# Where the norm factor enters at the recurrence layer and the last layer, and six queue orders

## The chip, the cores and the metric

The kernel runs on one core of a Trainium2 chip. The time is the device time of one execution in microseconds; less is better. Engines are named as in the profile: PE is TensorE, DVE VectorE, ACT ScalarE, POOL GpSimd, SP the sync engine, which issues most of the DMAs.

## The reference, cut to what matters

The input x is 256 tokens by 2048. A first block of two transformer layers (attention of three kinds, then an MLP) ends in an RMSNorm. A second block follows: layer 0, the recurrence layer (a gated linear recurrence beside a matrix memory), and layer 1, the last layer (a state-space layer, SSD), each behind an RMSNorm of its own, and one more RMSNorm at the end. All is in fp32.

```python
def rmsnorm_2(x, w):                        # rmsnorm is the same
    y = xf * lax.rsqrt(jnp.mean(xf * xf, axis=-1, keepdims=True) + EPS)
    return (y * w).astype(x.dtype)

def first_block(...):
    for l in range(2):
        h = rmsnorm(x, norm_mix[l]);  proj = h @ w_in[l];  ...attention...;  x = x + mix @ w_o[l]
        h = rmsnorm(x, norm_mlp[l]);  u = relu(h @ w_up[l]);  x = x + (u * u) @ w_down[l]
    return rmsnorm(x, norm_final)

def second_block(x, ...):
    # layer 0, the recurrence layer
    u = rmsnorm_2(x, e_norm) @ e_w_in;  x_l, x_m, z = split(u)
    y_l = rglru(causal_conv(x_l));  y_m = mlstm(silu(causal_conv(x_m)), x_m)
    x = x + (concat(y_l, y_m) * silu(z)) @ e_w_out
    # layer 1, the last layer
    u = rmsnorm_2(x, o_norm) @ o_w_in;  z, xbc, dt = split(u)
    y = ssd_scan(silu(causal_conv(xbc)), softplus(dt + dt_bias), ...) + d_skip * xs
    x = x + (rmsnorm_of_groups(y * silu(z)) * gnorm) @ o_w_out
    return rmsnorm_2(x, final_norm)
```

The factor of a norm is one number for each token, and the gain one for each feature. So `rmsnorm(x, g) @ W` is (x · g) @ W, with each token's row of the result times its factor.

## The kernel before, in words

**Products.** A product of two fp32 operands is made of three of rounded parts: hi·hi, hi·lo, lo·hi. Weights come from HBM in units of 1 MB (128 x 2048 numbers), each into one of four slots of `raw`. For each unit ACT writes the rounded part `whi` (`high_unit` L867, `high_parts` L983), DVE the rest `wlo` (`low_unit` L1449, `low_parts` L1442), and PE multiplies. The activations stand in `act0` and `act1`, transposed (features on the partitions, 256 tokens along the row), as a high and a low part. A group is two units and gives 256 columns of output for all tokens. It is 32 pairs of matmuls in `products()`: L2391 with `whi` against high and low activations (512 columns), L2393 with `wlo` against the high ones (256). The main part of a group lies in columns 0 to 255 of a PSUM bank pair and the minor part behind it; the eviction adds them. In the stages that add to x (`resid`) the activations are the stationary side and the weights stream (`block_products`, L2349 to L2351).

**Stages.** `stages()` (L103) lists them: for each of two layers attention and then w_up and w_down by turns, four times; `norm2`; the four parts of e_w_in, `xl`, `xm`, `zm`, `zl`, of 8 groups each; `e_mix` (heads of the matrix memory, then the product with e_w_out, 22 groups); `norm`; of o_w_in the parts `tail` (1 group), `x` (2), `z` (2), `bc` (8); then the stages `ssd` with g = 0 to 6, of 4 groups each, which project group g+1 while they compute group g of the state-space layer. After g = 3 a residual stage with the first half of o_w_out stands between them (`ssd_end`), and `ssd_out` ends the kernel with the other half.

Each engine has its own queue, written out by hand from the same list. What is written first in an engine's block is issued first, and a wait for a semaphore holds everything behind it in that queue.

**How x is turned.** At the norms inside the first block, PE transposes raw x (`turn_raw`, L2288) while the residual stage before it is still running: after each block p > 0 two turns, and the last two (6 and 7) inside group (0, 0) of the next stage. ACT writes the gained high part (`turned_high`, L973), DVE the low part (`turned_low`, L1614), and the factor enters later. At `norm2` and `norm`, it is different. There the whole factor comes first: squares of all x on ACT, their sums, roots and reciprocals on DVE and ACT (L1621 to L1643, L1173, L1174, L1178), then a diagonal matrix `xdiag` of the factors (L1646, L1647). `turn(i)` multiplies x by that diagonal, which turns and scales in one (L2278, eight matmul records a turn; i = 0 to 3 stand before the products, i = 4 to 7 inside group (0, 0)). ACT L1187 and DVE L1655 write the two parts into `act0`. `norm2` has two norms in a row (norm_final, then e_norm_2): the first gain is multiplied into x by DVE (L2030) in the last residual stage.

**Evictions.** DVE copies the minor part out of PSUM and adds it to the major part: L1958 and L1959 for `store`, L1973 and L1974 for `silu` and `gate_y`, `evacuate()` L1458 and L1459 in the `ssd` stages.

**The ssd stages on GpSimd.** In stage g GpSimd convolves the newly projected tiles (`conv_pair`, L690, L695, L698: two pairs of the stage, and in g = 1 and 2 another pair 7+g for a later one), multiplies them by their gates (`gate_pair`, L717), multiplies z by its gate (L852), and adds up the squares of the gated y for the norm over a group: `y_adds` (L707, L709) writes `osum`, which PE multiplies by ones in `y_sums` (L2331; for g = 3 and 6 PE sums straight from the squares, L2327). The squares themselves are made on ACT (`y_squares`, L908) from `gated_y` of DVE (L1509, L1515), and ACT's sigmoid of z (L880) stands before them in ACT's queue.

**The start.** ACT's queue first waits for `x_dma1`, the landing of the second part of x, issues the DMA of all gain and convolution columns (304 KB, L1120), and then evicts the first turned tiles (L973) and makes the high part of the first unit (L1123, L1125). DVE follows with L1614 and L1847, and PE begins its products at L2425.

Of the kernel before, what the change touches and what calls it, by code (L numbers as in the profile page):

```python
# [15 lines left out]
F32 = mybir.dt.float32  # L16
F32R = mybir.dt.float32r
ACT = mybir.ActivationFunctionType
ALU = mybir.AluOpType
# [84 lines left out]
def stages():  # L104

    out = [dict(kind="load")]
    for l in range(DEPTH):
# [12 lines left out]
    out.append(dict(kind="gemm", w=e_in, k0=0, c0=0, ng=8, act=0, evac="store", dst="wide_a", pre="xl"))  # L120
    out.append(dict(kind="gemm", w=e_in, k0=0, c0=D, ng=8, act=0, evac="store", dst="wide_b", pre="xm"))
    out.append(dict(kind="gemm", w=e_in, k0=0, c0=3 * D, ng=8, act=0, evac="silu", dst="wide_e", pre="zm"))
    out.append(dict(kind="gemm", w=e_in, k0=0, c0=2 * D, ng=8, act=0, evac="gate_y", pre="zl"))
    out.append(dict(kind="e_mix", w=e_out, ng=22))

    o_in, o_out = ("o_w_in_2", 0), ("o_w_out_2", 0)
    out.append(dict(kind="norm", gain=("o_norm_2", 0)))
    out.append(dict(kind="gemm", w=o_in, k0=0, c0=2 * N_DI + D + N_SSD_H - GC, ng=1, act=0, evac="store", dst="tail"))
    out.append(dict(kind="gemm", w=o_in, k0=0, c0=N_DI, ng=2, act=0, evac="store", dst="wide_b", pre="x"))
    out.append(dict(kind="gemm", w=o_in, k0=0, c0=0, ng=2, act=0, evac="silu", dst="wide_z", pre="z"))  # L130
    out.append(dict(kind="gemm", w=o_in, k0=0, c0=2 * N_DI, ng=8, act=0, evac="store", dst="wide_a", pre="bc"))
# [8 lines left out]
def number(out):  # L140
# [6 lines left out]
    for before, s in zip(out, out[1:]):  # L147
        if before.get("evac") == "resid":
            s["after_resid"] = True
        if s["kind"] != "gemm":  # L150
            continue
        if before["kind"] in ("norm", "norm2"):
            s["turns"] = True
        if before["kind"] in ("norm", "norm2") or before.get("evac") == "relu2":
# [6 lines left out]
def vector_rows():  # L161

    out = []
    for l in range(DEPTH):
# [5 lines left out]
            (("o_gnorm_2", 0), 32)]  # L170
# [95 lines left out]
def build(nc, A, out, pick=None):  # L266
# [3 lines left out]
    with ExitStack() as ctx:  # L270
# [39 lines left out]
        for key, shape in vector_rows():  # L310
            vectors[key] = (n_rows, shape)
            n_rows += shape
        columns = sb("columns", [P, n_rows])
# [33 lines left out]
        gain_row = o_raw[:, 0:8, :].rearrange("p a t -> p (a t)")  # L347
        junk = wide_1[:, 1, :, :].rearrange("p a t -> p (a t)").rearrange("p (c f) -> p c f", c=2)
        r_row = std[:, 1, :]
# [2593 lines left out]
```

## Time and profile before

| | |
|---|---|
| median of 3 runs | 3521.62 us (3520.26 to 3522.58) |
| the profiled execution | 3520.35 us |
| its span in the profile | 3518.6 us |
| PE busy | 3471.3 us, 99% |
| DVE busy | 2235.9 us, 64% |
| ACT busy | 1600.3 us, 45% |
| POOL busy | 663.0 us, 19% |
| moved from HBM | 622.13 MB, 177 GB/s over the span |

The profile is of one execution, taken by the hardware profiler. The span goes from the first to the last instruction that it recorded. PE is the engine that multiplies, and it is hardly ever idle. So the short places where it stands tell more than the shares; the view of waits lists them by the instruction that ended them.

### The profile page before, as it was taken

The numbers are of one execution on the slowest core, as the hardware profiler recorded it, in microseconds if no ns is written. First come the engines' busy times: TensorE is split into PE (matmuls) and PEld (weight loads), VectorE is DVE, ScalarE is ACT, GpSimd is POOL, SyncE is SP. The second block draws the span as 40 slices with busy tenths as digits, with TensorE's granted clock in tenths as the row PEclk, the third lists the DMA queues.
The fourth block names the chain that finished last, engine by engine and source line by source line (L and its number), as shares of the span: only waits on it lengthen the run. The fifth ranks groups of instructions, "written<-read, shape, count | busy, mean of one in ns | idle before, by whom it ended". The sixth has DMA issues, their size and how long they took to land. (4 is left out here: it accounts for less than half of the span.)

```text
span 3518.6 us, 44743 instructions
## 1 busy us (share of the span) xinstructions
PE 3471.3 (99%) x18296; PEld 2896.3 (82%) x18296; DVE 2235.9 (64%) x2155; ACT 1600.3 (45%) x1766; POOL 663.0 (19%) x551
## 2 busy tenths in 40 slices
PE   9999999999999999999999999999999999999999
PEld 7777888888887778888888878888888788777887
DVE  5666646464656677646464658866667476875786
ACT  5555333333344565333333445633454444553564
POOL 1221000000000221000000001560000069770560
PEclk9999999999999999999999999999999999999999
DMA  6344555555545354555555544455444455454554
GB/s 221 143 167 166 185 187 190 191 185 186 190 179 192 132 180 156 191 185 186 190 191 183 200 180 162 175 191 190 158 145 155 161 186 193 168 178 174 182 201 150
DMA packets 94783, 626.83 MB, mean 178 GB/s; under 512 B 10928, under 2 KB 13232, under 8 KB 21392
## 3 DMA queue, kind: packets, MB, share of 16 engines
q1 hardware_dynamic: 84096, 601.99, 46.9%
q0 software_dynamic: 3168, 11.41, 1.0%
q10 hardware_dynamic: 7344, 10.94, 0.9%
q8 instruction: 129, 2.11, 0.2%
q14 instruction: 46, 0.38, 0.0%
HBM read 622.13 MB, written 2.16 MB: 177 GB/s over the span
## 5 line engine op out<-in xcount | busy, mean ns | idle before, releaser
L2391 PE MATMUL ps<-act,whi 128*128 128x512 f32 x4384 | 1551.0, 396 | 1.8 <-DVE wlo L1442 1.8
L1442 DVE TENSOR_TENSOR wlo<-raw,whi 128x2048 fp32r<-128x2048 f32 x404 | 941.2, 2350 | 471.6 <-ACT whi L983 449.8
L2393 PE MATMUL ps<-act,wlo 128*128 128x256 f32 x4384 | 1233.7, 281 | 0.0
L2391 PEld LDWEIGHTS ps<-act,whi 128*128 128x128 f32 x4384 | 825.5, 188 | 198.8 <-issue 4.8
L983 ACT ACTIVATE whi<-raw 128x2048 fp32r<-128x2048 f32 x358 | 683.7, 1913 | 621.1 <-DMA raw<-in_w_down 309.2
L2393 PEld LDWEIGHTS ps<-act,wlo 128*128 128x128 f32 x4384 | 823.8, 188 | 0.8
L867 ACT ACTIVATE whi<-raw 128x2048 fp32r<-128x2048 f32 x211 | 402.1, 1913 | 267.9 <-DMA raw<-in_o_w_in 87.7
L1449 DVE TENSOR_TENSOR wlo<-raw,whi 128x2048 fp32r<-128x2048 f32 x165 | 389.4, 2365 | 149.3 <-ACT whi L867 149.2
L2349 PE MATMUL ps<-whi,act 128*128 128x512 f32 x1152 | 456.1, 396 | 0.0
L2350 PE MATMUL ps<-wlo,act 128*128 128x512 f32 x1152 | 455.4, 395 | 0.0
L2351 PE MATMUL ps<-whi,act 128*128 128x512 f32 x1152 | 455.4, 395 | 0.0
L2349 PEld LDWEIGHTS ps<-whi,act 128*128 128x128 f32 x1152 | 216.6, 188 | 52.6 <-issue 0.2
L2351 PEld LDWEIGHTS ps<-whi,act 128*128 128x128 f32 x1152 | 216.4, 188 | 52.5
L2350 PEld LDWEIGHTS ps<-wlo,act 128*128 128x128 f32 x1152 | 216.4, 188 | 52.2
L1239 ACT ACTIVATE act<-big 128x512 f32 (+1 forms) x64 | 40.4, 632 | 424.0 <-DVE big L1965 424.0
L728 POOL DMA_DIRECT2D wide_b<-in_bias_b x4 | 2.3, 566 | 804.6 <-DVE wide L1701 804.6
L2449 PE MATMUL ps<-act,whi 128*128 128x512 f32 x384 | 138.9, 402 | 0.0
L796 POOL DMA_DIRECT2D o_raw<-in_norm_final x1 | 0.6, 581 | 663.2 <-PE ps L2393 663.2
L1962 DVE COPY big<-ps 128x512 f32<-128x512 f32 x64 | 44.3, 692 | 122.4 <-PE ps L2393 122.4
L690 POOL TENSOR_SCALAR wide<-wide_b,columns 128x256 f32<-128x256 f32 x48 | 44.7, 938 | 352.3 <-DVE wide_b L1959 222.2
L2425 PE MATMUL ps<-whi,act 128*128 128x512 f32 x256 | 104.2, 407 | 5.3 <-DVE wlo L1847 4.4
L2451 PE MATMUL ps<-act,wlo 128*128 128x256 f32 x384 | 108.0, 281 | 0.0
(419 smaller groups left out, 4545.4 us busy)
## 6 DMA issues: line engine op xcount, KB each, us to landing
raw<-in_w_up SPq DMA_DIRECT2D x128, 1024.0 KB, 4.8
raw<-in_w_down SPq DMA_DIRECT2D x128, 1024.0 KB, 4.8
raw<-in_o_w_in SPq DMA_DIRECT2D x80, 1024.0 KB, 4.8
raw<-in_e_w_in SPq DMA_DIRECT2D x64, 1024.0 KB, 4.8
raw<-in_w_in SPq DMA_DIRECT2D x60, 1024.0 KB, 4.8
raw<-in_w_o SPq DMA_DIRECT2D x32, 1024.0 KB, 4.8
raw<-in_e_w_out SPq DMA_DIRECT2D x32, 1024.0 KB, 4.8
raw<-in_o_w_out SPq DMA_DIRECT2D x32, 1024.0 KB, 4.8
```

The source lines that it names most:

```text
L867: act.activation(whi[:, slot, :], raw[:, slot, :], ACT.Copy).then_inc(sem("hi_ready"), 1)
L983: act.activation(whi[:, slot, :], raw[:, slot, :], ACT.Copy).then_inc(sem("hi_ready"), 1)
L1442: dve.tensor_tensor(wlo[:, slot, :], raw[:, slot, :], whi[:, slot, :].bitcast(F32), ALU.subtract).then_inc(sem("lo_ready"), 1)
L1449: dve.tensor_tensor(wlo[:, slot, :], raw[:, slot, :], whi[:, slot, :].bitcast(F32), ALU.subtract).then_inc(sem("lo_ready"), 1)
L2349: pe.matmul(ps[:, b + th, :], a_hi, hi, start=(kt == 0), stop=False)
L2350: pe.matmul(ps[:, b + th, :], a_hi, lo, start=False, stop=False)
L2351: ins = pe.matmul(ps[:, b + th, :], a_lo, hi, start=False, stop=(kt == KT - 1))
L2391: pe.matmul(ps[:, b + f, :], whi[:, slot, w], a[:, kt, :, :].rearrange("p a t -> p (a t)"), start=(kt == 0), stop=False)
L2393: ins = pe.matmul(ps[:, b + f, S:2 * S], wlo[:, slot, w], a[:, kt, 0, :], start=False, stop=(kt == KT - 1))
L2425: pe.matmul(ps[:, b + th, :], a_hi, hi, start=(kt == 0), stop=False)
L2449: pe.matmul(ps[:, b + f, :], whi[:, slot, w], act0[:, kt, :, :].rearrange("p a t -> p (a t)"), start=(kt == 0), stop=False)
L2451: ins = pe.matmul(ps[:, b + f, S:2 * S], wlo[:, slot, w], act0[:, kt, 0, :], start=False, stop=(kt == KT - 1))
```

## The change

It has two parts.

**The factor enters late, also at the recurrence layer and the last layer.** The stages `norm2` and `norm` go. x is turned raw in the stage before (the last w_down for `xl`, `e_mix` for `tail`) with the gain as a column. For the recurrence layer the gains norm_final and e_norm_2 are multiplied together once, at the start. As in the first block, turns 6 and 7 stand in group (0, 0). Behind the products of group (0, 0) of `xl`, and of `tail`, PE waits for `diag` and makes a row of factors that is the same on every partition, ones x `xdiag`, in two matmuls. ACT copies it to `n_row` (which takes the place of `osum`). Each eviction of `xl`, `xm`, `zm`, `zl`, `x`, `z`, `bc` and of the `ssd` stages then multiplies by that row: DVE has a third operation; for `xl` and `xm` ACT copies the minor part (`minor_part`), so that DVE keeps two. The factor of `tail` is applied in `decay_inputs`. The factors themselves are computed beside group 0 (`paired_factors`, `single_factor`, `factor_diagonal`), between the units of ACT and DVE. GpSimd's sum of squares goes to `cos`, its gain row for norm_final to `wide_b`. The DMA of the columns stands behind turned_high(3) and waits for `x_dma3`; 8 KB with norm_final follow it.

**Six orders of the queues.** (1) The sigmoids of conv pairs 8 and 9 go on ACT from the end of their stage into the next. (2) `gate_pair(8)` and `(9)` go on GpSimd behind the products of z and `y_adds`. (3) `gated_y` stands ahead of `evacuate(g-1, 3)` on DVE. (4) `y_sums` stands later in PE's queue: in the middle of the second unit of `block_products` instead of behind the first, and in `ssd_out` inside the second instead of behind the first. (5) In `e_mix` each half of `head_products` waits for its own split, and the splits 0 and 1 are interleaved with the units. (6) `lru_scans` is made in two halves.

```diff
@@ stages
-            out[-1].update(squares=True, gain_row="norm_final", gained=True)
+            out[-1].update(squares=True, gain_row="norm_final", gained=True, turn_next=("e_norm_2", 0))
-    out.append(dict(kind="norm2", gain=("e_norm_2", 0)))
+    (xl: turned=("e_norm_2", 0), scaled_by="row"; xm, zm, zl, x, z, bc: scaled_by="row"; tail: turned=("o_norm_2", 0))
+    out.append(dict(kind="e_mix", w=e_out, ng=22, turn_next=("o_norm_2", 0)))
-    out.append(dict(kind="norm", gain=("o_norm_2", 0)))
@@ PE
                         products(s, p, c, acts[s["act"]], fresh)
+                        if s.get("turned") and s["evac"] == "store" and isinstance(p, int) and p == 0 and c == 0:
+                            pe.wait_ge(sem("diag"), 1 if s.get("pre") == "xl" else 2)
+                            pe.wait_ge(sem("x_low"), T["x_low"] + 2)
+                            for th in range(2):
+                                ins = pe.matmul(ps[:, 6, th * P:th * P + P], ones[:, :], xdiag[:, th, :], ...)
+                            ins.then_inc(sem("norm_row"), 1)
-                        if s.get("turns") and isinstance(p, int) and p == 0 and c == 0 and kt < 8 and kt % 2:
-                            turn(4 + kt // 2)
-                if k in ("norm", "norm2"):
-                    pe.wait_ge(sem("diag"), T["diag"] + 1)
-                    for i in range(4):
-                        turn(i)
+                        if s.get("ssd_end") and p == 0 and n == 1 and i == 1:        # block_products
+                            y_sums(s["ssd_end"])
-                    if s.get("ssd_end") and p == 0 and n == 0:
-                        y_sums(s["ssd_end"])
+                            if i == 1 and a == 1:                                      # ssd_out
+                                y_sums(g - 1)
-                        if i == 0:
-                            y_sums(g - 1)
-                        pe.wait_ge(sem("split"), h + 2 if part in "qk" else 5 + h)
+                        pe.wait_ge(sem("split"), h + 1 if part in "qk" else 5 + h)
+                            if a and part in "qk":
+                                pe.wait_ge(sem("split"), h + 2)
+                        if k in (24, 25, 29):                                          # e_mix
+                            i = {24: 0, 25: 2, 29: 4}[k]
+                            pe.wait_ge(sem("evacuated"), e_G0 + 16 + i)
+                            turn_raw(i, T["x_low"])
+                            turn_raw(i + 1, T["x_low"])
@@ ACT
+                    def minor_part(g):
+                        b = 2 * ((s["G0"] + g) % 2)
+                        act.wait_ge(sem("multiplied"), 2 * (s["G0"] + g) + 2)
+                        wait(act, sem("evacuated"), s["G0"] + g)
+                        act.activation(big[:, 0, :]..., ps[:, b:b + 2, S:2 * S], ACT.Copy).then_inc(sem("minor_in"), 1)
+                    def row_in():
+                        act.wait_ge(sem("norm_row"), 1 if s.get("pre") == "xl" else 2)
+                        act.activation(n_row, ps[:, 6, 0:S], ACT.Copy).then_inc(sem("norm_row_in"), 1)
+                        if s.get("pre") == "xl" and g == 0:
+                            high_unit(2 * s["G0"] + 2)
+                            gained_squares(3)
+                            high_unit(2 * s["G0"] + 3)
+                            act.wait_ge(sem("x_sum"), T["x_sum"] + 1)
+                            act.activation(rs[:, 2, :], yr[:, :], ACT.Sqrt).then_inc(sem("x_std"), 1)
+                            act.activation(rs[:, 0, :], rs[:, 1, :], ACT.Sqrt).then_inc(sem("x_r1"), 1)
+                        elif s.get("dst") == "tail":
+                            act.wait_ge(sem("x_sum"), T["x_sum"] + 1)
+                            act.activation(rs[:, 1, :], rs[:, 0, :], ACT.Sqrt, bias=eps[:, :], scale=1.0 / D)
+                            high_unit(2 * s["G0"] + 2)
+                            high_unit(2 * s["G0"] + 3)
-                        act.wait_ge(sem("x_dma1"), 32)                                 # before turned_high(0)
-                        act.dma_start(columns[:, KT:n_rows], ...)
+                        act.wait_ge(sem("x_dma3"), 32)                                 # after turned_high(3)
+                        act.dma_start(columns[:, KT:n_rows], ...).then_inc(sem("columns_in"), 16)
+                        act.dma_start(lru_c[:, 0, :], A["vectors"][:, n_rows:n_rows + KT]).then_inc(sem("final_in"), 16)
+                    if g in (2, 3):                                                    # ssd, behind high_unit(u + 5)
+                        conv_sigmoid(6 + g)
-                    if g in (1, 2):
-                        conv_sigmoid(7 + g)
@@ DVE
+                        elif s.get("pre") == "xl" and 2 * p + c == 0:
+                            gain_block(3, T["x_low"] - 6)
+                            low_unit(2 * s["G0"] + 2)
+                            paired_factors()
+                            factor_diagonal()
+                            low_unit(2 * s["G0"] + 3)
+                        elif s.get("dst") == "tail":
+                            single_factor()
+                            factor_diagonal()
+                            low_parts(s["G0"] + 1, p)
+                        if s.get("pre") in ("xl", "xm"):
+                            dve.wait_ge(sem("minor_in"), ...)
+                        elif s["evac"] != "relu2":
+                            own.then(dve.tensor_copy(t1, minor))
+                        if s.get("scaled_by"):
+                            own.then(dve.tensor_tensor(t2, major, t1, ALU.add))
+                            dve.wait_ge(sem("norm_row_in"), 1 if s["pre"] in E_AT else 2)
+                            if s.get("scaled_by"):
+                                ins = dve.tensor_tensor(to, t2, row2, ALU.mult)
@@ DVE, evacuate of the ssd stages
-                dve.tensor_tensor(to, ps[:, b:b + 2, 0:S], to, ALU.add).then_inc(sem("evacuated"), 1)
+                own.then(dve.tensor_tensor(to, ps[:, b:b + 2, 0:S], to, ALU.add))
+                dve.tensor_tensor(to, to, n_row.unsqueeze(1).broadcast_to([P, 2, S]), ALU.mult
+                                  ).then_inc(sem("evacuated"), 1)
@@ DVE, ssd, ssd_end and ssd_out
+                        gated_y(g - 1)
                         evacuate(g - 1, 3)
-                        gated_y(g - 1)
@@ POOL
-                pool.tensor_tensor(osum[:, :], squares[:, 0:S], squares[:, S:2 * S], ALU.add).then_inc(sem("s_add"), 1)
+                pool.wait_ge(sem("d_out"), 16)
+                pool.tensor_tensor(cos[:, :], squares[:, 0:S], squares[:, S:2 * S], ALU.add).then_inc(sem("s_add"), 1)
-                    if g in (1, 2):
-                        gate_pair(7 + g)
                     for m in (2 * g, 2 * g + 1):
                         ... y_adds, z ...
+                    if g in (1, 2):
+                        gate_pair(7 + g)
```

## Rows read from the trace of the kernel before

**Rows 1.** the page's busy time, share and instructions of each engine
```profile
PE 3471.3 (99%) x18296; PEld 2896.3 (82%) x18296; DVE 2235.9 (64%) x2155; ACT 1600.3 (45%) x1766; POOL 663.0 (19%) x551
```

**Rows 2.** TensorE's waits: line, releaser: us in total, times, longest us
```profile
PE ps L2331 <- POOL osum L709: 12.4, 2, 6.5
PE ps L2278 <- DVE xdiag L1647: 9.8, 2, 6.0
PE ps L2327 <- ACT staged L908: 3.7, 2, 1.9
PE ps L2391 <- DVE wlo L1442: 1.8, 3, 1.1
PE ps L2730 <- DVE act L1607: 1.8, 1, 1.8
```

**Rows 3.** timeline of the start: start us, us, engine, line, idle before
```profile
7.63 0.84 PE L2288 MATMUL ps<-ident,x 128*128 128x128 f32 x3
11.86 0.84 ACT L973 ACTIVATE act<-ps,columns 128x256 fp32r<-128x256 f32 x2 [9.18 <-DMA x<-in_x]
14.96 0.79 PE L2425 MATMUL ps<-whi,act 128*128 128x512 f32 x1 [4.41 <-DVE wlo L1847]
```

**Rows 4.** timeline, end of w_down to recurrence layer: TensorE, once VectorE
```profile
2101.18 0.40 PE L2351 MATMUL ps<-whi,act 128*128 128x512 f32 x1
...
2105.38 0.16 DVE L1628 TENSOR_REDUCE rs<-ss 128x2 f32<-128x8 f32 x1 [0.87 <-ACT big L1255]
...
2107.62 6.16 PE L2278 MATMUL ps<-xdiag,x 128*128 128x128 f32 x32 [6.05 <-DVE xdiag L1647]
2115.02 1.06 PE L2278 MATMUL ps<-xdiag,x 128*128 128x128 f32 x8
...
2129.05 0.47 PE L2391 MATMUL ps<-act,whi 128*128 128x512 f32 x1 [0.50 <-DVE wlo L1442]
```

**Rows 5.** timeline of TensorE, end of the mixing stage to the last layer
```profile
2791.95 5.36 PE L2278 MATMUL ps<-xdiag,x 128*128 128x128 f32 x32 [3.73 <-DVE xdiag L1647]
...
2811.93 0.40 PE L2391 MATMUL ps<-act,whi 128*128 128x512 f32 x1
```

**Rows 6.** timeline, attention to w_up handover: TensorE, VectorE
```profile
1381.72 1.04 PE L2288 MATMUL ps<-ident,x 128*128 128x128 f32 x8
1386.84 0.60 PE L2288 MATMUL ps<-ident,x 128*128 128x128 f32 x4
...
1392.00 4.49 DVE L1442 TENSOR_TENSOR wlo<-raw,whi 128x2048 fp32r<-128x2048 f32 x2 [0.92 <-ACT whi L983]
```

**Rows 7.** timeline of GpSimd in the recurrence stages
```profile
3008.37 2.67 POOL L709 TENSOR_TENSOR osum<-staged 128x256 f32<-128x256 f32 x1
...
3032.66 6.19 POOL L695 TENSOR_SCALAR wide<-wide_b,columns 128x256 f32<-128x256 f32 x2
...
3051.48 0.93 POOL L695 TENSOR_SCALAR wide<-wide_a,columns 128x256 f32<-128x256 f32 x2
...
3067.03 0.72 POOL L709 TENSOR_TENSOR osum<-staged 128x256 f32<-128x256 f32 x1
```

**Rows 8.** timeline of TensorE at the sums of y, g=0 and g=1
```profile
3011.29 0.60 PE L2331 MATMUL ps<-osum,ones 128*128 128x256 f32 x2
...
3067.81 1.22 PE L2331 MATMUL ps<-osum,ones 128*128 128x256 f32 x2 [5.92 <-POOL osum L709]
```

**Rows 9.** the same at the residual stage after g=3
```profile
3173.30 3.07 PE L2327 MATMUL ps<-staged,ones 128*128 128x256 f32 x8 [1.90 <-ACT staged L908]
```

**Rows 10.** one window of the bc stage: us, busy of each engine, granted clock
```profile
2900.00:2956.00 56.00, 56.00 (x319) 48.86 (x318) 30.48 (x20) 19.34 (x13) 53.46 (x49) 1.00 0.56 197
```

**Rows 11.** groups of VectorE and ScalarE by line: busy us, mean ns, idle
```profile
L1959 DVE TENSOR_TENSOR wide_a<-ps,big 128x512 f32<-128x512 f32 x5 | 3.5, 692 | 0.2
...
L1442 DVE TENSOR_TENSOR wlo<-raw,whi 128x2048 fp32r<-128x2048 f32 x404 | 941.2, 2350 | 471.6 <-ACT whi L983 449.8
...
L983 ACT ACTIVATE whi<-raw 128x2048 fp32r<-128x2048 f32 x358 | 683.7, 1913 | 621.1 <-DMA raw<-in_w_down 309.2
```

More of the change, by code:

```diff
@@ L130, in stages @@
-    out.append(dict(kind="gemm", w=o_in, k0=0, c0=0, ng=2, act=0, evac="silu", dst="wide_z", pre="z"))
-    out.append(dict(kind="gemm", w=o_in, k0=0, c0=2 * N_DI, ng=8, act=0, evac="store", dst="wide_a", pre="bc"))
+    out.append(dict(kind="gemm", w=e_in, k0=0, c0=0, ng=8, act=0, evac="store", dst="wide_a", pre="xl",
+                    turned=("e_norm_2", 0), scaled_by="row"))
+    out.append(dict(kind="gemm", w=e_in, k0=0, c0=D, ng=8, act=0, evac="store", dst="wide_b", pre="xm", scaled_by="row"))
@@ new lines, in stages @@
+    out.append(dict(kind="gemm", w=e_in, k0=0, c0=3 * D, ng=8, act=0, evac="silu", dst="wide_e", pre="zm",
+                    scaled_by="row"))
+    out.append(dict(kind="gemm", w=e_in, k0=0, c0=2 * D, ng=8, act=0, evac="gate_y", pre="zl", scaled_by="row"))
+    out.append(dict(kind="e_mix", w=e_out, ng=22, turn_next=("o_norm_2", 0)))
+    o_in, o_out = ("o_w_in_2", 0), ("o_w_out_2", 0)
+    out.append(dict(kind="gemm", w=o_in, k0=0, c0=2 * N_DI + D + N_SSD_H - GC, ng=1, act=0, evac="store", dst="tail",
+                    turned=("o_norm_2", 0)))
@@ L132, in stages @@
+    out.append(dict(kind="gemm", w=o_in, k0=0, c0=N_DI, ng=2, act=0, evac="store", dst="wide_b", pre="x",
+                    scaled_by="row"))
+    out.append(dict(kind="gemm", w=o_in, k0=0, c0=0, ng=2, act=0, evac="silu", dst="wide_z", pre="z", scaled_by="row"))
+    out.append(dict(kind="gemm", w=o_in, k0=0, c0=2 * N_DI, ng=8, act=0, evac="store", dst="wide_a", pre="bc",
+                    scaled_by="row"))
     for g in range(N_G - 1):
@@ L147, in number @@
     for before, s in zip(out, out[1:]):
-        if before.get("evac") == "resid":
+        if before.get("evac") == "resid" or before["kind"] == "e_mix":
             s["after_resid"] = True
@@ L151, in number @@
             continue
-        if before["kind"] in ("norm", "norm2"):
-            s["turns"] = True
-        if before["kind"] in ("norm", "norm2") or before.get("evac") == "relu2":
+        if before.get("evac") == "relu2":
             s["fresh"] = 2
@@ L1264, in _ @@
                                 gained_squares(g // 2 - 1)
-                        if s.get("gained"):
-                            gained_squares(3)
                     else:
@@ L2270, in _ @@
             T = Tally()
-            def turn(i):
-                wait(pe, sem("act_ready"), T["act_ready"] - 8 + i - 3)
-                for kt in range(2):
-                    for th in range(2):
-                        at = P * (2 * i + kt)
-                        ins = pe.matmul(ps[:, 4 + i % 4, kt * S + th * P:kt * S + th * P + P], x[:, th, at:at + P],
-                                        xdiag[:, th, :], start=True, stop=True)
-                ins.then_inc(sem("x_turned"), 1)
             def turn_raw(i, base):
@@ L2330, in y_sums @@
                     pe.wait_ge(sem("s_add"), g + 1 - sum(n < g for n in (3, 6)))
-                    ins = pe.matmul(ps[:, 7, 0:S], ones[:, :], osum[:, :], start=True, stop=True)
+                    ins = pe.matmul(ps[:, 7, 0:S], ones[:, :], cos[:, :], start=True, stop=True)
                 ins.then_inc(sem("s_ss"), 1)
```

237 lines of the change are left out of this document (112 added, 125 removed).

## The prediction

> **What bounds the kernel now.** I read the page's busy line first: TensorE is busy 99% of the span, VectorE 64%, ScalarE 45% [rows 1]. So the time can fall only where TensorE works without need, works slowly, or waits. The second view is its waits by releaser [rows 2]: 12.4 us for `osum` (two waits), 9.8 for `xdiag` (two), 3.7 for `staged`, 1.8 for `wlo` in a group, 1.8 for the low half of `act` where the mixing layer begins; 4.4 more pass before the first product [rows 3]. Nearly all of these are places that the diff touches. The timeline then shows that a wait costs more than its length: the two records of the sums take 0.60 us where nothing was waited for and 1.22 behind a wait of 5.92 [rows 8], and eight of them behind a wait of 1.90 are listed with 3.07 [rows 9], 0.38 each. The reader should see that TensorE, once it has stood, goes on at about half its pace for some records; I put 0.8 to 1 us of slow restart on each long stall.
>
> The profiled execution took 3520.35 us, span 3518.6; the median of the runs shown is 3521.62, 1.3 above it. I sum against 3520.35.
>
> **Handover to the recurrence layer.** Before, the last product of w_down starts at 2101.18 (next slot 2101.41), TensorE stands 6.05 us until `xdiag` is there, runs four turns cold (32 records, 6.16 us), then group 0 with four more turns in it, and group 1 starts at 2129.05 after 0.50 us for `wlo` [rows 4]. That is 27.64 us. After, three pairs of raw turns lie in the last residual stage, whose products hide the evictions. Turning is still work: the row of eight raw records has 1.04 us, 0.25 of it the overlap of the last record's end with the next matmul, so 0.79, and 0.08 of restart for the slower first product: 0.87 a pair, 2.6 for three. Turns 6 and 7 lie inside group 0, four records each (0.60 less 0.25, and 0.08: 0.43 each) [rows 6]. A turn of the old kind keeps TensorE 1.06 less 0.25, and 0.08, so 0.89 [rows 4]; the group with four of them runs from 2797.06 (2791.95 + 5.36 - 0.25) to 2811.93, 14.87 [rows 5]. So a bare group is 11.3, and with the two raw turns 12.15. Its twin in the attention layer had no stall, and VectorE there was free for the low weights at 1392.00, 9.5 us into its group [rows 6]. New is that TensorE waits for `diag` behind group (0,0) to make the factor row. The chain of factors hangs on the last block of x: today it is done 6.2 us after the last product (2107.62 less 2101.41). Now two `high_unit`s of 1.91 us [rows 11] stand ahead of the last squares and the roots on ScalarE, and turned_low and low_units stand ahead of the factors on VectorE. An estimate: low unit from 9.5 us into the group (as in the twin), 2.35 long, then the chain of factors, 2105.38 to 2107.62 by today's rows [rows 4], 2.2 to 2.4: 14.3, 2.2 behind the end of the group. What is queued behind that wait is all of TensorE: group 1. Bounds: 0 if the factors come at the 6.2 of today, 4.5 if one more low unit of 2.35 [rows 11] stands in front of the 2.2. Row and slow restart: 1.0. Sum 2.6 + 12.15 + 2.2 + 1.0 = 17.95: gain **9.6** (6 to 12.3).
>
> **Handover to the last layer.** The wait of 3.73 before 2791.95 began at 2788.22; the last record's end overlaps by 0.16, so the next slot was 2788.06. From there to 2811.93 are 23.87 us [rows 5]. After: 2.6 + 12.15 + 0.45 for the row (the factor needs only one sum, one root, one reciprocal, so it is not waited for) + 0.7 for a late low unit, the price of the wait before (0.50) and its restart = 15.9. Gain **8.0** (6 to 8.6). The raw turns wait for m_std, m_abs, m_h, which free their PSUM; below them in the queue is only the output product, and the norms are long done.
>
> **Start.** TensorE begins at 14.96, 4.41 us late, behind the first low weights. These wait for ScalarE's high ones, and ScalarE's first activation comes at 11.86, though the first turned tiles were there at 8.47 (7.63 + 0.84) [rows 3]: it stands at the wait for x_dma1, ahead of the columns' DMA. With that DMA moved behind turned_high(3), it can begin up to 11.86 - 8.47 = 3.4 earlier, and TensorE with it, near 11.6, if raw0 is in by then. About 0.4 returns at the next units, whose transfers end when they did. The columns land later, and they are first waited for at t = 13 and 14 of the first projection's loop, on VectorE and ScalarE; the new load of norm_final is on the same queue and 8 KB. Gain **3.0** (0, if raw0's landing is what comes last, to 5, if the slow beginning is shorter too).
>
> **Order changes.** (a) Mixing layer: the wait of 1.8 [rows 2] goes, since the first head needs only one split, and the second follows under four steps of products; with its restart **2.5** (0.5 to 2.7). (b) Splits and units interleaved: the longest wait for `wlo`, 1.1 [rows 2], is of this kind: **1.1** (0 to 1.3). (c) y_sums in the residual stage after g=3 sits 1.5 products' blocks later: the wait of 1.9 with 0.15 around it, about 1.0 of slow records (3.07 for eight, where two warm ones have 0.60 with the overlap [rows 8]) and 0.95 in the block behind: **4.0** (2 to 4.5) [rows 9]. (d) The same in ssd_out: **1.6** (0 to 2.3), the other half of the 3.7 [rows 2].
>
> (e) y_adds in stages g=1 and 2. TensorE stood 5.92 and 6.50 (rows 2 give 12.4), until GpSimd's `osum` at 3067.03 + 0.72 = 3067.75 [rows 7, 8]. The queue ahead is one chain of convolutions and gates on GpSimd. The order takes one gate pair (some 2 us) out of the front, but the second convolution starts from an eviction that comes 2.1 us later by three third operations. Both nearly cancel. I take **+1.3**; ends -3 and +13.9 (both waits and their restarts gone).
>
> **The third operation of the evictions.** zm, zl, x, z, bc and the recurrence evict in three VectorE operations, not two (the add is 0.69 [rows 11], the copy like it), 16 + 12 + 28 = 56 evictions; xl and xm leave the copy to ScalarE. For the multiply, whose inputs both lie in SBUF, the nearest rows are the add of the same 512 columns, 0.69, and the low unit, of that kind but four times as wide, 2.35, so 0.59 for 512 [rows 11]. I take 0.69, for 39 us of VectorE in all. Beside it is room: in bc VectorE is busy 30.5 of 56 us, 5.1 us idle a group [rows 10]. Where it hurts is the narrow slack: in g=0 the adds end at 3011.04 and TensorE's product starts at 3011.29 [rows 7, 8]. I count five places of about 0.6 (0.69 less part of such a slack), and 0.4 in xl: **-3.4**. Ends: only xl's -0.4, and two operations, 1.38, at each of the five, -7.3.
>
> The Trainium skill speaks against this edit: its page "SBUF — State Buffer", section "Who interferes with whom", says that a VectorE instruction with two SBUF inputs shuts out a GpSimd one that reads SBUF, while one with at most one SBUF input doesn't. What is seen here agrees: the same pair of `L695` takes 6.19 us beside the low units and 0.93 at another time [rows 7]. The old copy and add have one SBUF input at most; the new multiply has two. By the rule the GpSimd chain loses the operation's length each time and more; by the bare row it loses nothing, as GpSimd is held by VectorE's order alone. The result is a rival below.
>
> **Sum.** 9.6 + 8.0 + 3.0 + 2.5 + 1.1 + 4.0 + 1.6 + 1.3 - 3.4 = 27.7. 3520.35 - 27.7 = 3492.7, forecast **3493** (own range 3485 to 3499, from the bounds of the two handovers and the start).
>
> **Rivals.** (1) The GpSimd chain really comes free: both waits of (e) go with their restarts, 13.9 for 1.3, and the time is 3480. For it: the waits are just 6 us, and gates go out of the front. Against: the gates that leave are 2 us of that queue. Chance 0.15. (2) The handovers give half: `diag` is late by a further group's work, 17.6 becomes 8.8, 3502. For it: two high units and several VectorE jobs stand ahead of the factors. Against: the chain itself is only 2.2 us and one low unit more is 2.35. Chance 0.12. (3) The third operation delays GpSimd's adds in five recurrence stages (0, 1, 2, 5, 6), three operations of 0.69 each and as much again by blocking (as 6.19 to 0.93 suggests is possible), 2.8 us each = 14 in the place of 1.3 - 3.4: 3520.35 - 29.8 + 14 = 3505. By the slack of 0.25 in g=0 it starts to matter at once. Chance 0.12. (4) Slower: the 39 us of third operations land on TensorE as each group waits for its eviction, 39 against 29.8 gained: 3529.5. It decides where VectorE has less than 0.69 idle in a group; bc with 5.1 [rows 10] is far from it. Chance 0.04. (5) The change doesn't do what it says: handovers and orders gain nothing (17.6 and 10.5 go), as new waits stand where the old ones did: 3520.8. Against it: the diagonal turns are 16 groups of records that are gone whatever follows. Chance 0.02. The forecast keeps 0.55.
>
> **How the numbers follow.** The forecast's own range covers most of its 0.55. To leave no more than 2 in 10 out, I reach to rival (1) at 3480 and to (2) and (3) at 3502 to 3505: 3480 to 3505. A measurement of this kernel can tell about 0.2%, 7 us, from no change. Faster by more than that (under 3514.6): the forecast, (1), (2), (3), 0.94. Within it 0.02, (5); slower 0.04, (4).
>
> **What would show it.** After w_down: three x8 rows of raw turns in the stage, two x4 rows in group 0, and a wait for `diag` of about 2 us, then two matmuls of ones. If it is over 6, rival 2. The wait for `osum`'s successor (`cos`) should still stand twice at 5 to 6 us; if it is gone, rival 1; if five appear, rival 3. The first product should start near 11.6. The waits for `staged` and for `act` should be missing. The multiply should be a row of about 0.69 with 48 or more records. A TensorE busy time that fell much less than its waits and turns did would mean that the slow clock after stalls was mis-sized, and the sum would be wrong.

## The result and the profile after

The changed kernel takes 3544.76 us (median of 4 runs, 3544.11 to 3546.62), the one before 3521.99 (median of 4). The ratio is 1.0064 with a 95% interval of 1.0051 to 1.0077: 23 us slower, where 28 us faster had been forecast, and outside the range. The profiled execution has a span of 3543.4 us, 24.9 more than before.

Page of the changed kernel, busy time of the engines (the view of rows 1):

```profile
PE 3478.1 (98%) x18240; PEld 2893.9 (82%) x18240; DVE 2278.2 (64%) x2213; ACT 1608.9 (45%) x1786; POOL 669.6 (19%) x551
```

Its waits of TensorE by releaser (the view of rows 2):

```profile
PE ps L2398 <- ACT sq L933: 19.9, 7, 3.7
PE ps L2330 <- issue: 9.6, 2, 5.7
PE ps L2362 <- POOL cos L707: 7.9, 5, 3.0
...
PE ps L2422 <- DVE wlo L1457: 2.7, 5, 1.1
...
PE ps L2772 <- DVE wide L2093: 2.0, 1, 2.0
PE ps L2358 <- ACT staged L905: 1.8, 1, 1.8
PE ps L2726 <- DVE xdiag L1676: 1.7, 1, 1.7
PE ps L2923 <- DVE wlo L1464: 1.6, 1, 1.6
```

The waits for `xdiag` before the turns and for `staged` in the middle have gone, as meant. But 19.9 us of a new kind head the list: L2398 is the product of the recurrence gates (`lru_gates`), seven times behind ScalarE's sigmoids of the gates (L933). TensorE's waits for GpSimd's sums, 12.4 us before, have become 7.9, and 9.6 us before L2330 have joined them, a wait that no row has a releaser for.

Where the time went is best read from the starts of the groups of products, found by counting the matmuls of `products()` and of the residual stages in both traces. The shift is the time after less the time before; a negative change is a gain. Each trace is of one execution.

| stretch | change, us | shift at its end | forecast |
|---|---|---|---|
| start | -2.4 | -2.4 | -3.0 |
| last w_down and handover, to group 1 of xl | -10.5 | -12.9 | -9.6 |
| rest of xl, xm to its group 1 | **+34.0** | +21.1 | +0.4 |
| xm to its group 4 | -0.3 | +20.8 | -1.1 |
| rest of xm, zm, zl to its last group | +2.3 | +23.2 | 0 |
| mixing stage, to behind its waits | -1.3 | +21.8 | -2.5 |
| e_w_out with its turns, handover to group 0 of x | -8.1 | +13.7 | -8.0 |
| x, z, bc, ssd g=0, to the sums after it | +3.2 | +16.9 | third operations: +3.0 over all ssd stages |
| to the sums after ssd g=2 | +5.4 | +22.4 | -1.3 |
| ssd g=3, residual stage to its second block | -3.1 | +19.3 | -4.0 |
| residual stage, ssd g=4 to 6 | +2.8 | +22.1 | in the +3.0 |
| ssd_out | +2.8 | +24.9 | -1.6 |

The 2.3 us of zm and zl are not the change's. No wait stands there, and the granted clock is 1.00 in all the traces, but a group takes 11.31 us where it took 11.17. e1 below, with the same code in these stages as the changed kernel, has 11.17, and e3, which has it too, 11.31. So a trace can differ by some 2 us from another here for a cause that stays open.

Handover to the recurrence layer, timeline of TensorE in the changed kernel (the view of rows 4):

```profile
2105.81 0.60 PE L2319 MATMUL ps<-ident,x 128*128 128x128 f32 x4
2107.66 0.60 PE L2319 MATMUL ps<-ident,x 128*128 128x128 f32 x4
...
2115.66 0.71 PE L2726 MATMUL ps<-xdiag,ones 128*128 128x128 f32 x4 [1.74 <-DVE xdiag L1676]
...
2144.36 3.15 PE L2398 MATMUL ps<-wide,staged 128*128 128x256 f32 x8 [3.66 <-ACT sq L933]
```

Two raw turns of four records stand in group 0, and behind it the row product waits 1.74 us for `xdiag`. Then the lines to learn from, the same stretch of ScalarE:

```profile
2132.81 1.92 ACT L982 ACTIVATE whi<-raw 128x2048 fp32r<-128x2048 f32 x1 [0.59 <-DMA raw<-in_e_w_in]
2140.74 0.60 ACT L1174 ACTIVATE big<-ps 128x512 f32<-128x512 f32 x1 [6.00 <-PE ps L2424]
2141.35 1.28 ACT L931 ACT_TABLE_LOAD   x1
2142.64 0.47 ACT L931 ACTIVATE wide<-ps,columns 128x256 f32<-128x256 f32 x1
...
2143.73 0.48 ACT L933 ACTIVATE sq<-ps,columns 128x256 f32<-128x256 f32 x1
...
2148.40 1.91 ACT L982 ACTIVATE whi<-raw 128x2048 fp32r<-128x2048 f32 x1 [4.19 <-PE ps L2398]
```

ScalarE is idle for 6.00 us until TensorE has ended the group, copies the minor part in 0.60, loads the sigmoid's table in 1.28 and only then computes the sigmoids, of which the last ends at 2144.2. TensorE stands 3.66 us for it, and its eight gate records behind the wait have 3.15 us, where eight had 1.89 in the kernel before. The window says the same with the clock:

```profile
2130.00:2250.00 120.00, 101.14 (x493) 85.18 (x492) 79.89 (x119) 57.65 (x72) 0.00 (x0) 0.90 0.39 137
```

101 of 120 us busy at a granted clock of 0.90: the product's engine idles a sixth of the time in xl and xm, and is slow in a part of the rest. Over all seven waits, and over a like stretch of the kernel before:

```profile
2116.00:2254.00 138.00, 118.08 (x579) 99.86 (x578) 96.50 (x136) 67.81 (x87) 8.22 (x6) 0.90 0.40 144
```

```profile
2130.00:2240.00 110.00, 110.00 (x610) 95.97 (x610) 99.51 (x138) 70.16 (x84) 11.21 (x5) 1.00 0.50 180
```

Here are both halves of the 34 us. TensorE stands for 19.9 us of the 138. The granted clock of 0.90 costs a tenth of them, about 14 us more: it falls to the lower of its two levels (1.2 in place of 2.4 GHz) behind each wait (0.58 from 2144.4 to 2148.3, after the wait of 3.66) and is back at 0.99 from 2148.3 on. That is 2 us of slow work for each wait of about 3.

### The profile page after: what moved, and what is told of

Its sections match the earlier page's. It is cut to its first block and busy times, and to the rows that moved or that the text cites. A ratio compares the mean times of both kernels' runs of the same rounds, so it can differ in the third digit from the quotient of the medians.

```text
span 3543.4 us, 44787 instructions
## 1 busy us (share of the span) xinstructions
PE 3478.1 (98%) x18240; PEld 2893.9 (82%) x18240; DVE 2278.2 (64%) x2213; ACT 1608.9 (45%) x1786; POOL 669.6 (19%) x551
## 5 line engine op out<-in xcount | busy, mean ns | idle before, releaser
L2380 PE MATMUL ps<-whi,act 128*128 128x512 f32 x1152 | 456.0, 396 | 0.8 <-DVE act L1549 0.8
L2382 PE MATMUL ps<-whi,act 128*128 128x512 f32 x1152 | 455.1, 395 | 0.0
L687 POOL TENSOR_SCALAR wide<-wide_b,columns 128x256 f32<-128x256 f32 x48 | 63.8, 1335 | 377.5 <-DVE wide_b L2003 254.4
L695 POOL TENSOR_TENSOR wide<-wide 128x510 f32<-128x510 f32 (+2 forms) x72 | 111.5, 1549 | 6.0
```

Of the source, the lines that this page charges most:

```text
L695: ins = pool.tensor_tensor(room[:, :, d:S], room[:, :, d:S], tap[:, :, 0:S - d], ALU.add)
L2380: pe.matmul(ps[:, b + th, :], a_hi, hi, start=(kt == 0), stop=False)
L2382: ins = pe.matmul(ps[:, b + th, :], a_lo, hi, start=False, stop=(kt == KT - 1))
```

## The experiments

Four questions, nine kernels: what made the 34 us, what the third operations cost in the ssd stages, what the orders do, and what paces the stages g=1 and 2. Each kernel was timed beside the one before on the same chip, and its shifts are taken from its trace in the way of the table above. There were three chips: e1 to e4 ran on one, e5 to e8 on another, e9 on a third. The medians of before were 3521.2, 3521.7 and 3521.8, 0.6 us apart. A kernel's one trace need not be of its median run: those of e2, e3 and e7 are 2.9, 6.5 and 4.7 us faster than it, that of e5 2.1 slower.

**e1_gates_first.** The sigmoids go ahead of the copy.

```diff
+                        if at in GATES_AT:
+                            lru_sigmoids(GATES_AT.index(at))
                         minor_part(g)
```

> The changed kernel, with ScalarE's sigmoids of the recurrence gates put ahead of its copy of the minor part in the groups of xl and xm; nothing else differs. Theory A (order of a queue): the copy waits for the end of the group's own products, so the sigmoids behind it come after them, and TensorE, whose next gate product needs them, stands after each of seven groups; the shift of xl and xm against the kernel before (from -12.9 to +21.1 us, 34 us) goes nearly whole: 3544.8 - 31 to 34 = 3511 to 3514 us, and no wait of TensorE for sq is left. Rival B (ScalarE's copy itself is the load: the eviction waits for it, VectorE and the next group follow): the wait moves to the eviction, at least 15 of the 34 us stay, 3526 us or more.

Measured 3517.12 us (ratio 0.9989, 0.9979 to 0.9998). TensorE's waits for sq:

```profile
PE ps L2399 <- ACT sq L933: 2.8, 2, 1.4
```

and ScalarE's sigmoids in the same place:

```profile
2136.60 1.92 ACT L982 ACTIVATE whi<-raw 128x2048 fp32r<-128x2048 f32 x1 [0.72 <-DMA raw<-in_e_w_in]
2138.53 1.28 ACT L931 ACT_TABLE_LOAD   x1
2139.82 0.48 ACT L931 ACTIVATE wide<-ps,columns 128x256 f32<-128x256 f32 x1
...
2140.91 0.48 ACT L933 ACTIVATE sq<-ps,columns 128x256 f32<-128x256 f32 x1
2144.37 0.60 ACT L1172 ACTIVATE big<-ps 128x512 f32<-128x512 f32 x1 [2.98 <-PE ps L2425]
```

They run while TensorE multiplies, and the copy alone waits for it. From group 1 of xl to group 1 of xm 5.6 us are lost (shift -11.6 to -6.0), where the changed kernel lost 34; e3 below, with the same code here, loses 3.2. Theory A holds and B falls. The time came 3 to 6 us above the expectation: two waits of 1.4 are left, each in a group after one with the roots, 7 us of ScalarE that now start behind the copy's wait and push the next high units and sigmoids back; and `xdiag` was 3.5 us late in this execution, where the changed kernel, e2 and e3 have 1.7.

**e2_dve_copies.** VectorE copies the minor part in xl and xm, as before the change.

```diff
-                        if s.get("pre") in ("xl", "xm"):
-                            minor_part(g)
-                        if s.get("pre") in ("xl", "xm"):
-                            dve.wait_ge(sem("minor_in"), ...)
-                        elif s["evac"] != "relu2":
+                        if s["evac"] != "relu2":
                             own.then(dve.tensor_copy(t1, minor))
```

> The changed kernel with the minor parts of xl and xm copied by VectorE (three operations an eviction) in place of ScalarE. Theory A: the waits for the sigmoids go as well, 34 us, but VectorE, busy 80 of 89 us in this stretch before, takes 16 x 0.69 = 11 us more, of which 4 to 11 reach TensorE: 3515 to 3523 us. Rival B: the loss in xl and xm is one of the third operation or of the gate chain itself and stays where VectorE copies: 3540 us or more.

Measured 3514.12 us (0.9982, 0.9973 to 0.9992). No wait for sq is left, and the window over xl and xm shows what the third operation costs there:

```profile
2115.00:2225.00 110.00, 109.87 (x609) 95.96 (x610) 102.94 (x147) 71.51 (x86) 8.86 (x4) 1.00 0.51 182
```

VectorE is busy 102.9 of 110 us, TensorE 109.9 at full clock. The shift is -13.4 at group 1 of xl and at group 1 of xm: nothing is lost, and the time is 0.9 us under the expectation. So I had also misread VectorE's room: 94% busy, in operations that TensorE doesn't wait for, was still enough, and the copy on ScalarE, which was to spare VectorE, was the whole damage.

**e3_ssd_two_ops.** As e1, without the multiplication in `evacuate` (the scale is missing in the ssd stages).

```diff
-                own.then(dve.tensor_tensor(to, ps[:, b:b + 2, 0:S], to, ALU.add))
-                dve.tensor_tensor(to, to, n_row..., ALU.mult).then_inc(sem("evacuated"), 1)
+                dve.tensor_tensor(to, ps[:, b:b + 2, 0:S], to, ALU.add).then_inc(sem("evacuated"), 1)
```

> As e1_gates_first, and in the ssd stages the eviction leaves out the multiplication by the factor row (two operations as before; the scale is missing there). From bc's end to the end of the kernel the changed kernel lost 8 us against the one before though the sums after g=3 came 2.8 earlier, so 10.8. Theory C: these come from the third operation, through GpSimd's chain of convolutions (each starts later and runs slower beside VectorE): 9 to 11 us faster than e1_gates_first, 3501 to 3505 us. Rival D: they come from the new orders of the queues: within 2 us of e1_gates_first.

Measured 3510.43 us (0.9968, 0.9956 to 0.9979), 6.7 under e1 by the medians, and so 5 to 9 us above the expectation and short of its 9 to 11; e3's runs lie up to 7.5 us apart, and the traced one is the fastest. The traces leave out what differs ahead of the ssd stages: from the first group of bc to the end e1 loses 8.6 us (shift -11.3 to -2.7) and e3 gains 1.4 (-15.1 to -16.5), 10.0 between them. Over the same stretch the other kernels with three operations and the convolutions in their old place lose 9.4 (the changed one) and 11.2 (e2), and those with two, e4 and e8 below, gain 1.0 and lose 1.1. So the 28 third operations of the ssd stages cost 7 us by the medians and about 10 by the traces, and rival D falls. The path that theory C names carries less than half: 4.2 of the 10.0 lie between the sums after g=0 and those after g=2, where GpSimd's convolutions are late, and 5.8 are spread over the other stages.

**e4_orders_only.** Before, with the six orders alone.

> The kernel before with the six orders of the queues alone; the norms stay as they were. Theory C: the orders gain where they are meant to: mixing stage 2.5, splits 1.1, sums after g=3 and in ssd_out 5.6, GpSimd's chain 2 (a gate of 1.3 to 2.5 us less in front of it, twice): 9 to 12 us faster than before, 3510 to 3513 us. Rival D: the orders are what costs in the ssd stages: no faster than before minus 3, 3518 us or more.

Measured 3518.99 us (0.9995, 0.9986 to 1.0005), not distinguishable from before; its trace is 2.7 shorter. By its number rival D holds, by its mechanism neither: the sums after g=3 gained 3.8, and up to the last layer 1.6 came, but TensorE's waits in g=1 and 2 came to 12.1 us (with three short ones in other stages 13.3) where there were 12.4, though a gate had left GpSimd's front. GpSimd in g=1, with six orders:

```profile
3054.10 4.97 POOL L695 TENSOR_SCALAR wide<-wide_a,columns 128x256 f32<-128x256 f32 x2
3059.15 1.08 POOL L698 TENSOR_TENSOR wide<-wide 128x506 f32<-128x506 f32 x1
3060.19 2.49 POOL L717 TENSOR_TENSOR wide_b<-wide 128x512 f32<-128x512 f32 x2
```

and VectorE beside it:

```profile
3053.11 0.69 DVE L1461 TENSOR_TENSOR wide_b<-ps,wide_b 128x512 f32<-128x512 f32 x1
3053.72 4.63 DVE L1444 TENSOR_TENSOR wlo<-raw,whi 128x2048 fp32r<-128x2048 f32 x2
```

The last two taps take 4.97 us beside a pair of low units. Before, VectorE stood for 5 us in that place, since ScalarE's next high unit was queued behind its wait for GpSimd's convolution 8. Order (1) takes that wait away, VectorE has work, and GpSimd is held.

**e5_orders_2to6.** As e4, with `conv_sigmoid(7 + g)` where it was.

> The kernel before with orders (2) to (6); only the sigmoids of conv pairs 8 and 9 stay where they were on ScalarE. With all six, TensorE's waits in g=1 and 2 came to 13.3 us, against 12.4 before, though a gate is gone from the front. Theory E: the sigmoid's wait for GpSimd held back ScalarE's next high units, so VectorE had a hole of 5 us in which GpSimd ran its last taps at full speed (1.8 us against 5.0 beside a pair of low units); with the sigmoid back the hole is back, and the gate still gone: these waits come to 7 to 10 us and the time is 3 to 6 us under that of all six orders, 3513 to 3516. Rival F: the place of the sigmoid is nothing to GpSimd: within 1.5 us of all six, 3519.

Measured 3514.28 us (0.9976, 0.9966 to 0.9987). The same rows of GpSimd and VectorE:

```profile
3055.89 0.94 POOL L695 TENSOR_SCALAR wide<-wide_a,columns 128x256 f32<-128x256 f32 x2
3056.91 1.08 POOL L698 TENSOR_TENSOR wide<-wide 128x506 f32<-128x506 f32 x1
3057.95 2.56 POOL L717 TENSOR_TENSOR wide_b<-wide 128x512 f32<-128x512 f32 x2
```

```profile
3054.90 0.69 DVE L1461 TENSOR_TENSOR wide_b<-ps,wide_b 128x512 f32<-128x512 f32 x1
3061.01 5.09 DVE L1444 TENSOR_TENSOR wlo<-raw,whi 128x2048 fp32r<-128x2048 f32 x2 [5.42 <-ACT whi L867]
```

0.94 us for the same two taps, with VectorE idle 5.42. TensorE's five waits for `osum` sum to 10.3, 8.8 of them in g=1 and 2, and no wait before the bases is left. The bases are the products of TensorE that `ssd_bases` writes ahead of the sums. The median is 4.7 us under e4's, as theory E has it, but on another chip, and the intervals of the ratios touch (0.9986). Between the sums after g=0 and those after g=2 the traces show 4.5 us less: e5 gains 3.1 there, e4 loses 1.4. An order that lets one engine work sooner made another slower, and that other one was the pacer.

**e7_before_convs_late and e6_after_convs_late.** Conv pairs 8 and 9, needed only from g=4 and g=6 on, leave the stages g=1 and 2 and are made at the end of g=3, where GpSimd was idle; in e7 on the kernel before, in e6 on e2. The edit of e7, shortened:

```diff
-        CONV_SEQ = [0, 1, 2, 3, 4, 5, 6, 7, 10, 11, 12, 13, 8, 14, 15, 9] + list(range(16, 24))
+        CONV_SEQ = list(range(8)) + list(range(10, 18)) + [8, 9] + list(range(18, 24))
+            if n in (8, 9):                                     # conv_room
+                return wide_a[:, 8 * (n - 8):8 * (n - 8) + 2, :], wide_a[:, 8 * (n - 8) + 2:8 * (n - 8) + 4, :]
-                    if g in (1, 2):
-                        conv_pair(7 + g)
-                    if g in (1, 2):
-                        gate_pair(7 + g)
+                    if g == 3:
+                        pool.wait_ge(sem("s_cb"), 4)
+                        conv_pair(8);  conv_pair(9);  gate_pair(8);  gate_pair(9)
+                            if s.get("ssd_end") and g in (3, 5):              # ScalarE
+                                conv_sigmoid(8 if g == 3 else 9)
```

> The kernel before with conv pairs 8 and 9 at the end of stage g=3, nothing else. Theory G: both waits for osum (5.9 and 6.5) and their restarts go, 13 to 14 us: 3507 to 3509 us. Rival H: half or less of it goes, 3514 or more.

> As e2_dve_copies, and conv pairs 8 and 9 (with their gates) are taken out of the stages g=1 and 2 and made on GpSimd at the end of stage g=3, beside the residual stage, where GpSimd was idle; their rooms are tiles of wide_a that are no longer used. Theory G (GpSimd's chain of convolutions paces g=1 and 2): 14 to 19 us of GpSimd work leave each of these two stages, the two long waits of each (about 15 us in all with their slow restarts) go: 3514 - 12 to 16 = 3498 to 3502 us. Rival H (something else, such as the squares or z's sigmoid on ScalarE, comes just behind it): 3514 - 5 or less, 3509 or more.

e7 measured 3506.53 us (0.9957, 0.9941 to 0.9974), 0.5 us under theory G's range, e6 3498.31 (0.9939, 0.9923 to 0.9956), within it. In e7's waits no row of GpSimd's sums is left. The chain of convolutions is what paces these two stages, with the change and without. In e6 five waits for the sums stay, 1.1 to 1.8 us each:

```profile
PE ps L2362 <- POOL cos L709: 7.4, 5, 1.8
...
PE ps L2380 <- DVE act L1551: 3.1, 1, 3.1
```

**e8_only_recurrence_layer.** As e2, the last layer's norm as before.

```diff
-    out.append(dict(kind="e_mix", w=e_out, ng=22, turn_next=("o_norm_2", 0)))
-    (tail turned; x, z, bc scaled_by="row"; third operation in evacuate)
+    out.append(dict(kind="e_mix", w=e_out, ng=22))
+    out.append(dict(kind="norm", gain=("o_norm_2", 0)))
```

> As e2_dve_copies, but the last layer has its norm as in the kernel before: diagonal turns, evictions of two operations in x, z, bc and ssd; the late factor is at the recurrence layer alone. Theory C: the handover's gain there, 7.1 us, goes, and with it the cost of the third operations (10 in the ssd stages, 1.7 in x, z and bc): 3514 - 4.6 = 3509 to 3511 us. Rival I: the third operations cost less than the handover gives, where both are on: 3516 us or more.

Measured 3508.49 us (0.9959, 0.9945 to 0.9973), 5.6 under e2, 0.5 us under theory C's range. e2 ran on another chip, the intervals touch (0.9973), and the spans of the two traces are only 1.7 apart, e2's being of its fastest run. Alone this pair would leave it doubtful that at the last layer the late factor costs more than it gives; e9 against e6 says the same, more clearly.

**e9_recurrence_convs_late.** Both together.

> As e8_only_recurrence_layer (late factor at the recurrence layer alone, VectorE copying in xl and xm, the six orders) with conv pairs 8 and 9 at the end of stage g=3. Theory G: the waits of g=1 and 2 that are left in e8 (6.9 and about 5 of the 6.8, with restarts) go: 3508.5 - 12 to 16 = 3493 to 3497 us, the fastest so far, and some 3 us under e6_after_convs_late. Rival J: with GpSimd no longer the pacer the third operations of the ssd stages cost little, so that the full change (e6, 3498 us) is as fast or faster: 3497 to 3501 us.

Measured 3492.06 us (3490.64 to 3495.69; ratio 0.9914, 0.9900 to 0.9927): 29.8 us faster than before on the same chip and the fastest of all. That is 1 us under theory G's range and 6 us under e6 (3498.31), where some 3 were expected; rival J falls. The two were timed on different chips, and the intervals just overlap (0.9927, 0.9923), but the traces agree: from the first group of bc to the end e9 gains 14.9 us and e6 3.7. So the third operations cost 11 us also where GpSimd's convolutions no longer pace g=1 and 2. Its waits of TensorE are short:

```profile
PE ps L2329 <- DVE xdiag L1679: 3.5, 1, 3.5
...
PE ps L2800 <- DVE wide L2107: 2.0, 1, 2.0
...
PE ps L2382 <- POOL cos L709: 1.6, 5, 0.4
```

The same five waits for the sums, 7.4 us in e6 with three operations, are 1.6 here with two.

## Why the prediction was wrong

**The step that failed.** The prediction says of the third operation "xl and xm leave the copy to ScalarE" and books 0.4 us for both stages. It priced the copy by VectorE's time and never asked what stands behind its wait in ScalarE's queue. The copy waits for the end of the group's own products; behind it stand the sigmoids of the gates; TensorE's next gate product, written right behind these same products, waits for them. So TensorE waited for an engine that was waiting for TensorE, seven times, and 34.0 us were lost in all: 19.9 of standing and about 14 of the lower clock behind it. That second part is 2 us a wait, where the prediction allows 0.8 to 1 us of slow restart on a long stall. e1 and e2 show the cause from two sides: with the order mended 3 to 6 us are lost, with the copy gone nothing. With this term at 0.4 the changed kernel would have been 8.7 us faster than before (24.9 - 33.6 = -8.7 by the spans), 3511 to 3512 us: still outside the range, which ends at 3505.

**The second step that failed** is the third operations of the ssd stages together with the sums, (c) to (e). From x to the end the forecast gains 3.9 us, and the changed kernel lost 11.2 (shift +13.7 to +24.9). More on it below. The prediction's own range has a slip too: the bounds it names (handovers 6 to 12.3 and 6 to 8.6, start 0 to 5) give 3487 to 3501, not 3485 to 3499.

**The handovers.** Right. To the recurrence layer 10.5 us came for 9.6 forecast: three pairs of turns in the last w_down (TensorE is shifted by 0.8 to 0.9 at each, 2.6 in all, for 2.6), 1.74 us of waiting for `diag` where I had 2.2. Rival (2) is out. At the last layer, group 0 with the row behind it took 13.1 (2812.54 to 2825.65) for 13.3; with three pairs of turns, 2.6, that is a gain of 8.2 for 8.0 (8.1 by the shifts).

**Order (a).** The wait of 1.8 for `act` at its start has gone, and 2.0 stand at L2772 for VectorE's `wide` instead, with the restart. Over the stage 1.3 came for 2.5, and e7, which has the order of before there, shows 1.3 too, so no gain of the order can be told from these traces. I had named the wait that goes, not the one that is late next.

**Order (b).** The wait of 1.1 was not one at the splits. It stood in xm (2257.18), behind VectorE's four scans of the recurrence, 4.21 us in a piece:

```profile
2250.40 4.21 DVE L1581 TENSOR_TENSOR_SCAN wide_a<-wide_a,wide 128x256 f32<-128x256 f32 x4
2254.53 4.70 DVE L1442 TENSOR_TENSOR wlo<-raw,whi 128x2048 fp32r<-128x2048 f32 x2
```

In e4 the scans stand there in halves, by order (6), the wait is gone, and 1.3 us come. The prediction's size was right for another order than the one it named.

**Start.** 2.4 for 3.0; the first product is at 11.98 (11.6 forecast), and the next unit's wait gives some back. The size is not settled to better than 1 us: e5 and e7, which don't touch the start, have 0.9 and 1.2 there.

**The sums (c) and (d).** After g=3: 3.1 in the changed kernel and 3.8 in e4, for 4.0; in the changed kernel 0.8 came back as a wait for the activations. In ssd_out 2.8 were lost where 1.6 of gain stood. In e4 the wait for `staged` is down to 0.3 there, so the moved sums do what was meant, but 1.6 of waiting for low weights has come in its place, which I had not looked for; and with the third operations in front the wait for `staged` is back at 1.8.

**Third operations, (e) and rival (3).** I took 3.4 us lost and 1.3 gained. The ssd stages show about 10 for the third operation (e3), in the place of five times 0.6. The rival's mechanism is seen: in g=1 the second convolution started 1.4 us later and then ran 5.4 us longer beside VectorE (33.5 us from start to gates for 28.1), and TensorE stood twice, 5.66 before the bases and 1.68 before the sums, as it did in g=2 with 3.9 and 3.0:

```profile
3082.95 1.19 PE L2330 MATMUL ps<-wide_a 128*128 128x256 f32 x2 [5.66 <-issue]
...
3087.95 1.22 PE L2362 MATMUL ps<-cos,ones 128*128 128x256 f32 x2 [1.68 <-POOL cos L707]
```

This second place I had missed: the bases wait for GpSimd's gates (`cv_out`) just as the sums do, a step earlier. Before, the gates were done about 1 us ahead of them. In the other stages, g=0, 4 and 5, TensorE waits 1.0 to 1.3 us for the sums in the changed kernel and 0.2 to 0.7 in e3 and e4, so the operation reaches it there without a late convolution. The sign that I had set for this rival, five waits for `cos`, doesn't tell: five stand in e4 as well, where an eviction has two operations, only shorter. How the 10 us divide between the wait, the restart and the activations that come late in e6 stays open. As to the Trainium skill, "SBUF — State Buffer", section "Who interferes with whom": the direction is as it says, a GpSimd operation that reads SBUF is held while VectorE runs one with two SBUF inputs; e4 and e5 show the same two taps with 4.97 and 0.94 us. The multiply itself has 0.69 us at the least and 0.84 on average in the ssd stages, 1.81 at most, where the add before it, which reads PSUM, has 0.69 in all 28; I had taken 0.69. That the added multiply, and not the low units that it shifts, did the holding, these runs don't separate.

**Chances.** 0.04 for slower was too little. The price of rival (4) was 39 us for VectorE's operations reaching TensorE in every group, and that mechanism never came: in e2 VectorE was busy 94% of xl and xm, and once the factor row was made TensorE waited nowhere for it. What came was a wait in a queue, by chance of about the same size, on an engine at 45% of busy time.

## What to carry to other kernels

A step moved to an idle engine brings its wait along: list what is queued behind that wait, and who waits for those, above all if the engine waited for is among them. Here that loop cost 34 us for sixteen copies of 0.60 us, and the engine it spared had room. And when an order is mended, look at what the freed engine then collides with: the time is set by the slowest chain (here GpSimd's convolutions), so the first thing to ask is which of its links can go where that engine is idle.

## What the runs showed of the hardware

Seven waits of TensorE, 2.2 to 3.7 us each and 19.9 in all, were followed by stretches at the lower clock: 0.90 was granted over the 138 us, where a like stretch of the kernel before has 1.00, which cost about 14 us more. A table load for the sigmoid is shown with 1.28 us, and it lies on the path where ScalarE's wait does. GpSimd's pair of `tensor_scalar` over 128x256 took from 0.93 to 6.19 us, by what VectorE did beside it; 5 us of an idle VectorE were worth about 4 us of GpSimd. The same product group of TensorE took 11.17 us in some stages and executions and 11.31 in others, at a granted clock of 1.00 in both; the cause is open.
